# The causal mask of the plain heads' later query tiles: added by VectorE in PSUM, not by TensorE

## What is computed

```python
s = jnp.einsum('bqghd,bkgd->bghqk', qr, kwc) * scale
kp = t0 - WIN + jnp.arange(Q_BLOCK + WIN)
diff = t[:, None] - kp[None, :]
p_w, _, _ = masked_softmax_stats(s, (diff >= 0) & (diff < WIN) & (kp[None, :] >= 0))
o_w = jnp.einsum('bghqk,bkgd->bqghd', p_w.astype(vwc.dtype), vwc)
```

## Time and profile before

| | |
|---|---|
| three runs | 1239.37, 1239.57, 1242.0 us; median 1239.57 |
| the profiled execution | 1240.52 us, span 1238.7 us, mean granted clock 0.997 |
| TensorE matmul busy | 1206.8 us, 97% |
| TensorE weight load busy | 980.4 us, 79% |
| VectorE busy | 595.9 us, 48% |
| ScalarE busy | 398.8 us, 32% |
| GpSimd busy | 179.1 us, 14% |
| plain items | about 451 to 635 us of the span |

### The profile page before, as it was taken

How to read it: one execution, slowest core, us unless ns; L and a number is a source line. 1 busy time by engine, 2 the same in 40 slices (tenths; PEclk the granted TensorE clock), 3 DMA queues, 4 the chain that set the end, 5 groups by cost and what they waited for, 6 DMA issues and landing times.

```text
span 1238.7 us, 15847 instructions
## 1 busy us (share of the span) xinstructions
PE 1206.8 (97%) x6163; PEld 980.4 (79%) x6163; DVE 595.9 (48%) x883; ACT 398.8 (32%) x568; POOL 179.1 (14%) x200
## 2 busy tenths in 40 slices
PE   6999999999999998999999999999999999999997
PEld 5888888888888877876667788888888888888886
DVE  4544444453333646577776644454444444442222
ACT  4323223222223223433334543334233223222222
POOL 3100000000002661445643000002000000000000
PEclk9999999999999999999999999999999999999998
DMA  6333333223336521213112123333242233323331
GB/s 186 101 101 102 102 102 93 75 85 94 94 104 184 143 76 43 61 39 75 42 39 65 35 60 94 94 102 102 77 126 84 87 100 102 91 70 94 95 91 69
DMA packets 211168, 110.73 MB, mean 89 GB/s; under 512 B 31968, under 2 KB 207520, under 8 KB 211120
## 3 DMA queue, kind: packets, MB, share of 16 engines
q1 hardware_dynamic: 206736, 104.97, 29.5%
q0 software_dynamic: 4128, 4.93, 1.5%
q10 hardware_dynamic: 256, 0.17, 0.0%
HBM read 104.93 MB, written 2.10 MB: 86 GB/s over the span
## 4 chain that ended last, share of the span: by engine, by line
PE 85%; DVE 8%; ACT 3%; issue 2%; DMA 1%; SPq 0%; DVEq 0%; ACTq 0%
PE ps L1197 20%; PE ps L1198 20%; PE ps L1199 20%; PE ps L1284 6%; PE ps L1285 6%; PE ps L1286 6%; DVE w_lo L855 2%; ACT probs L719 1%; DVE stat L1020 1%; ACT w_hi L636 1%; PE ps L1399 1%; DVE probs L1054 1%; PE ps L1362 1%; DVE probs_t L1071 1%; PE ps L1379 1%
## 5 line engine op out<-in xcount | busy, mean ns | idle before, releaser
L855 DVE TENSOR_TENSOR w_lo<-w_raw,w_hi 128x2048 fp32r<-128x2048 f32 (+5 forms) x117 | 227.2, 1943 | 406.1 <-ACT w_hi L636 405.9
L1197 PE MATMUL ps<-xg_hi,w_hi 128*128 128x512 f32 x992 | 392.4, 396 | 6.3 <-DVE pool L987 5.0
L1199 PE MATMUL ps<-xg_hi,w_lo 128*128 128x512 f32 x992 | 387.3, 390 | 0.0
L1198 PE MATMUL ps<-xg_lo,w_hi 128*128 128x512 f32 x992 | 387.3, 390 | 0.0
L636 ACT ACTIVATE w_hi<-w_raw 128x2048 fp32r<-128x2048 f32 (+3 forms) x106 | 184.3, 1738 | 333.4 <-PE ps L1199 210.6
L1197 PEld LDWEIGHTS ps<-xg_hi,w_hi 128*128 128x128 f32 x992 | 186.7, 188 | 55.6 <-issue 16.3
L1199 PEld LDWEIGHTS ps<-xg_hi,w_lo 128*128 128x128 f32 x992 | 186.8, 188 | 39.4
L1198 PEld LDWEIGHTS ps<-xg_lo,w_hi 128*128 128x128 f32 x992 | 186.9, 188 | 37.5
L1284 PE MATMUL ps<-p_hi,w_hi 128*128 128x512 f32 x352 | 137.0, 389 | 0.0
L1286 PE MATMUL ps<-p_hi,w_lo 128*128 128x512 f32 x352 | 136.9, 389 | 0.0
L1285 PE MATMUL ps<-p_lo,w_hi 128*128 128x512 f32 x352 | 136.9, 389 | 0.0
(11 more groups left out here) (181 smaller groups left out, 1224.2 us busy)
## 6 DMA issues: line engine op xcount, KB each, us to landing
w_raw<-in_ffn_w_in SPq DMA_DIRECT2D x88, 512.0 KB, 4.6
w_raw<-in_w_in SPq DMA_DIRECT2D x32, 512.0 KB, 4.7
w_raw<-in_ffn_w_out SPq DMA_DIRECT2D x32, 384.0 KB, 3.3
w_raw<-in_ffn_w_out SPq DMA_DIRECT2D x32, 320.0 KB, 3.7
w_raw<-in_w_in SPq DMA_DIRECT2D x24, 256.0 KB, 3.6
w_raw<-in_w_out SPq DMA_DIRECT2D x8, 512.0 KB, 3.9
x_nat<-in_x SPq DMA_DIRECT2D x8, 256.0 KB, 4.4
w_raw<-in_w_branch_nsa SPq DMA_DIRECT2D x8, 256.0 KB, 3.8
```

The lines of the kernel that those rows point to most:

```text
L855: lo = V.tensor_tensor(w_lo[:, s, c], w_raw[:, s, c], w_hi[:, s, c].bitcast(F32), ALU.subtract)
L1197: mm(out, ah, bh, start=(first and i == 0), stop=False)
L1198: mm(out, ah, bl, start=False, stop=False)
L1199: last = mm(out, al, bh, start=False, stop=(final and i == len(pairs) - 1))
```

## The change

For the plain items with qt > 0 (24 of the 32), the two mask matmuls are gone, and the last score matmul closes the accumulation and raises `scores_psum`. VectorE adds the mask to the two diagonal blocks in one operation of 128 partitions by 2 by 128, in place in PSUM, with the bf16 mask read twice, before it takes the maximum; it waits for the addition's end. The items with qt = 0, the compressed and the dilated ones keep their mask matmuls.

```diff
@@ dve_prepare
             nk = (it[3] + 1) * P
             if it[0] == "nsa":
+                if it[3]:
+                    diagonal = ps[:, b:b + 2, nk - P:nk]
+                    link(dve, V.tensor_tensor(diagonal, diagonal, causal_b.unsqueeze(1).broadcast_to([P, 2, P]), ALU.add))
                 link(dve, V.tensor_reduce(stat[:, e, 0, 0:2], ps[:, b:b + 2, 0:nk], AX.X, ALU.max))
@@ pe_scores
                     last = mm(ps[:, b + g, 0:nk], pool[rows, Q_ROPE + hh, qt * P:qt * P + P], pool[rows, keys, 0:nk],
-                              start=(qt > 0), stop=(qt == 0))
-                if qt:
-                    last = add_masks(diagonal, causal_b)
+                              start=(qt > 0), stop=True)
                 last.then_inc(scores_psum, 1)
```

## The result

The changed kernel takes 1251.12 us (median of 4 runs, 1249.60 to 1251.73), the kernel before in the same comparison 1240.78 (4 runs, 1239.37 to 1242.08). The ratio is 1.0088, 95% interval 1.0076 to 1.0100: slower by 10.3 us by the medians, 10.9 by the ratio. I had forecast slower by 7.6. The sign, the price of an addition and the first third of the walk (the forecast's sum, followed item by item) hold; the sum is 2.7 us short.

A forecast was written before the change was run, and what follows sets the result against it. The chain was taken to alternate between TensorE legs and VectorE/ScalarE rounds. 15 additions on it cost 6.8 us; legs -0.3, -0.6, +0.45, +1.25 made +7.6 us, 1247.2 us on the median 1239.57; range 1243.0 to 1251.6.

The forecast's parts named there:

- What bounds the kernel: Between 460 and 635 us the chain alternates: four legs on TensorE, between them VectorE and ScalarE.
- TensorE bounds all of it: Rival for the whole kernel: all 24 mask pairs are won, 5.3 us, giving 1234.3 us; chance 0.05.
- VectorE hides it: Rival: most additions fall into VectorE's waits for TensorE, so the time stays within 1 us; chance 0.07.
- What is removed: 48 mask matmuls in 24 items, 0.22 us a pair, 5.3 us of TensorE, worth something only on TensorE's legs.
- The price of the addition: VectorE's in-place PSUM mask addition takes 0.424 us, 0.45 us an item with the gap; 24 items.
- The legs: Four TensorE legs with mask pairs, longer engine counting: 459-471 us -0.3, 508-522 -0.6, 558-563 +0.45, 581-612 +1.25 us.
- the leg at 558 us: 558-563 us, one pair: VectorE waits nowhere for TensorE, so the addition lies bare, +0.45 us and not -0.22.
- The leg at 581 us: 581-612 us, three pairs: a near tie; three additions less one 0.11 us wait, +1.25 us and not -0.66.
- Nothing else moved: Changed kernel's profile: beyond the listed changes in additions, matmuls, busy times, waits and chain legs, nothing else moves.
- Nothing after 635 us is changed ..., so a delay there goes to the end in full.: The chain crosses 635 us on VectorE, so the delay gathered by then reaches the end whole.
- The granted clock is 1.00.: Between 460 and 635 us in the kernel before, the granted clock is at the 2.4 GHz level.
- TensorE's waits: Between 460 and 635 us TensorE's waits for VectorE rise from 9 to some 22 us.

The follow-up runs named there:

- the kernels with 15 and with 24 additions: 15: only items 5-8, 15-17, 21, 23-25, 32-35 masked by VectorE, the rest by TensorE, 1251.29 us, ratio 1.0090 to the kernel before; 24: the changed kernel, 1251.12 us.
- the kernel with two additions: The changed kernel with VectorE's mask addition made twice for each of the 24 items; 1262.99 us, ratio 1.0185 to the kernel before.
- the kernel with both masks: The kernel before with VectorE's addition added and TensorE's mask matmuls kept, so the mask is added twice; 1251.29 us, ratio 1.0094.
- the four waits filled: The changed kernel with two matmuls on zeros in each of four TensorE waits (steps 5, 20, 24, 33); 1250.36 us, ratio 1.0087 to the kernel before.

## Why the prediction was right in sign and short in size

- *What bounds the kernel.* Right. "TensorE bounds all of it" would have given 1234.3 us, "VectorE hides it" no change.
- *What is removed.* 0.22 us a pair and the places where it counts are about right (0.63, 0.66, 0.1 and 0.4 us in the legs, without any mask). But nothing of it reached the end: without any mask the ratio is 1.0009, with an interval that leaves out the expected 0.9989. One clock drop (1.5 us) and one hold (1.05) took it up.
- *The price of the addition.* Right: 0.425 us against 0.424, and 0.45 with what stands between. Items 6, 7, 8, 16 and 17 come later by 0.46, 0.46, 0.47, 0.45 and 0.47 us one after the other.
- *The legs.* -0.3 and -0.6 were measured as -0.33 and -0.63. The one addition on the leg at 558 us lay bare as I said (+0.46, item 22). The leg at 581 us gave 0.78 and not 1.25, since two holds of before, 1.21 us at 604.55 and 0.84 at 607.61, shrank to one of 0.73. I had said that the chain would run on VectorE in both: from 587 to 620 us it now does (TensorE has 2% of it, before 98%), at 562 to 568 it doesn't, since TensorE with half its clock bounds again. And both terms stood on near ties that only the holds had made; without the rotation's work they are gone.
- *"Nothing else moved": VectorE's other operations keep their durations.* This is the step that failed: a term that the sum put at nothing without a reason. I had seen that L1049 took 1.36 us at 560.33, had set it beside L987 "while GpSimd works beside it", and used it only to choose the addition's price. I then let every other operation of VectorE keep its length while I moved it by 1 to 8 us against GpSimd's rotations. A delay moves the holds to other operations: 1.01 us became 2.53 behind item 17, 1.08 became 2.67 behind item 26. These two make +3.0 us of the walk; at item 35 it was short by 2.2, since smaller holds, met before and not after, gave some back. With the rotation's work left out no operation is held and the change costs 5.0 us.
- *"Nothing after 635 us is changed ..., so a delay there goes to the end in full."* The first half is true of the code and false of the time: 2.2 us more came between items 35 and the seventh dilated one, 1.66 of them from a rotation whose DMA was waited for 2.00 us.
- *"The granted clock is 1.00."* True of the kernel before, and I let it stand for the changed one: 0.97 in the stretch, by the three of the four drops that lie in it. They explain why TensorE is as busy as before with 5 us less to do; of the time they explain little, 0 us at the drop at 483, 1.5 at the one at 562, of which half was lost again one item later.
- *TensorE's waits* went from 10 to 18 us and not to 22; part of the delay is TensorE's own slower matmuls.
- *The range* (1243.0 to 1251.6) holds the median, near its upper end, by luck: the end stood for 24 additions at 0.50 us with no pair won, the additions took 0.425, and the surplus is in holds that no term of the sum had.

What stays open: why the holds fall worse in the changed kernel is told by rows for the three jumps, but that it must be so is not shown. The same walk with a delay of another size could have met other operations, and the kernels with 15 and with 24 additions arrive at the same time by different jumps.

## What to carry to other kernels

When a delay is walked down a chain, list which operations on it last longer than their twins, and find the engine beside them that makes them so. Their length belongs to the moment and not to the operation, so it must not be carried along with the shift, and a tie that such an operation makes is no tie. Here that put an uncertainty of 3 us on a sum of 7.6. Cutting the neighbour's instructions into shorter ones brought 4 us by the traces and 7 by the medians, where the edit at its best, by the rival in which TensorE bounds everything, could have brought 5.3.

## What the runs showed of the hardware

VectorE's operations with PSUM input didn't vary beside GpSimd. The cases that met one of its rotation operations are few, but all agree: L987 three times in the kernel before, 0.68 to 0.69 us against 0.686 in the mean; L1015 twice, 0.424 and 0.425; the new addition L1022 once in the kernel after, 0.433 (all 24: 0.418 to 0.433), and four times in the kernel with two additions, 0.416 to 0.433. Meanwhile the TENSOR_TENSOR and TENSOR_SCALAR operations on SBUF, down to a single column, were held by up to 1.7 us (1.72 in the kernel with both masks). Reductions from SBUF (L1039, met twice, 0.406 and 0.421 us) and reciprocals (L1048, met nine times, 0.15 to 0.17) were not. With GpSimd's operations cut to 2 columns no hold is left. The Trainium skill ("SBUF — State Buffer", Who interferes with whom) says that VectorE and GpSimd share one port pair as an exclusive lock for the whole instruction: an operation with two SBUF inputs, or in a two-port mode, contends, and one with at most one SBUF input outside these modes does not. The traces agree on these groups, and on the ends (538.96 against 538.92 us). GpSimd loses too: L591 took 2.10 us at 679.41 beside L855 and 1.29 at 540.90. Where the rule and the runs part is in its grain: in pieces of 0.46 us a hold of 1.20 us still occurred.

In the kernel after the granted clock fell to the 1.2 GHz level at waits of TensorE of 1.9 to 2.6 us, for some 3.4 us each time. The length of a single wait doesn't settle it: a wait of 2.02 us at 628 us brought no drop in the same kernel, and without any mask the clock fell at a wait of 0.98 us (491 us). With the four waits filled it fell elsewhere (493 and 629 us), at places where the kernel after had kept 2.4 GHz.
